# Input projection from x before its division by the row rms, with 1/rms applied by VectorE

## The reference

```python
def rmsnorm(x, g):
    xf = x.astype(jnp.float32)
    y = xf * lax.rsqrt(jnp.mean(xf * xf, axis=-1, keepdims=True) + EPS)
    return (y * g.astype(jnp.float32)).astype(x.dtype)
...
        u = rmsnorm(h, pre_mix_g[i])
        proj = u @ w_in[i]
        q, k, v, u_pool, u_conv = jnp.split(proj, splits, axis=-1)
...
        o_attn = stick_breaking_attention(q.reshape(heads), k.reshape(heads), v.reshape(heads))
        o_pool = multiscale_pool(u_pool, w_pool[i], pool_scale[i])
        o_conv = conformer_conv(u_conv, w_dw[i], b_dw[i], conv_ln_g[i], conv_ln_b[i], w_pw[i])
```

## Time and profile before

| | us |
|---|---|
| Runs, median of 3 | 1078.55 (1078.52 to 1079.44) |
| Span of the profiled execution, first to last instruction | 1076.4 |
| Median less that span | 2.15 |
| TensorE busy | 1065.8 (99%) |
| VectorE busy | 875.0 (81%) |
| ScalarE busy | 589.9 (55%) |

### The profile page before, as it was taken

The page is one execution under the profiler, slowest core; times in us unless marked ns, Lnnn a source line. Parts: engine busy times, 40 slices in busy tenths (PEclk is TensorE's granted clock), DMA queues, the critical chain, the costliest instruction groups (busy, mean ns, idle before and its releaser), DMA issues. The chain is left out here.

```text
span 1076.4 us, 15278 instructions
## 1 busy us (share of the span) xinstructions
PE 1065.8 (99%) x5757; PEld 923.4 (86%) x5757; DVE 875.0 (81%) x1113; ACT 589.9 (55%) x724; POOL 27.2 (3%) x46
## 2 busy tenths in 40 slices
PE   9999999999999999999999999999999999999996
PEld 8999999999888888888888888888888888888885
DVE  6699987637646887899899998998998888777787
ACT  6554454736555566565565555655555555554553
POOL 4000001101000000000000000000000000000000
PEclk9999999999999999999999999999999999999999
DMA  8655535444386485665756665666657666656554
GB/s 277 211 177 169 165 117 158 138 137 138 115 298 215 136 276 185 223 195 177 234 179 194 213 194 182 213 186 224 190 182 228 217 202 199 198 195 217 199 198 180
DMA packets 113207, 208.05 MB, mean 193 GB/s; under 512 B 9184, under 2 KB 46496, under 8 KB 111856
## 3 DMA queue, kind: packets, MB, share of 16 engines
q1 hardware_dynamic: 111952, 201.49, 58.9%
q10 hardware_dynamic: 608, 4.20, 0.9%
q0 software_dynamic: 576, 1.40, 0.4%
HBM read 202.86 MB, written 4.19 MB: 192 GB/s over the span
## 5 line engine op out<-in xcount | busy, mean ns | idle before, releaser
L550 ACT ACTIVATE w_hi<-raw 128x1024 fp32r<-128x1024 f32 x326 | 341.6, 1059 | 263.6 <-PE ps L1703 173.1
L903 DVE TENSOR_TENSOR w_lo<-raw,w_hi 128x1024 fp32r<-128x1024 f32 x326 | 395.1, 1227 | 97.2 <-ACT w_hi L550 96.6
L1701 PE MATMUL ps<-w_hi,uf 128*128 128x512 f32 x524 | 205.3, 392 | 0.1
L1703 PE MATMUL ps<-w_hi,uf 128*128 128x512 f32 x524 | 204.1, 389 | 0.0
L1702 PE MATMUL ps<-w_lo,uf 128*128 128x512 f32 x524 | 203.9, 389 | 0.0
L1365 PE MATMUL ps<-u,w_hi 128*128 128x272 f32 (+1 forms) x544 | 158.8, 292 | 0.0
L1367 PE MATMUL ps<-u,w_hi 128*128 128x272 f32 (+1 forms) x544 | 155.9, 287 | 0.0
L1368 PE MATMUL ps<-u,w_lo 128*128 128x272 f32 (+1 forms) x544 | 155.7, 286 | 0.0
L834 ACT CAST t_hi<-tx 128x1024 fp32r<-128x1024 f32 x84 | 87.0, 1048 | 56.0 <-DVE tx L1203 28.6
L1703 PEld LDWEIGHTS ps<-w_hi,uf 128*128 128x128 f32 x524 | 98.4, 188 | 20.7
L1701 PEld LDWEIGHTS ps<-w_hi,uf 128*128 128x128 f32 x524 | 98.4, 188 | 20.4 <-issue 0.5
(11 more groups left out here) (273 smaller groups left out, 1427.1 us busy)
## 6 DMA issues: line engine op xcount, KB each, us to landing
raw<-in_w_gate SPq DMA_DIRECT2D x176, 256.0 KB, 3.0
raw<-in_w_up SPq DMA_DIRECT2D x176, 256.0 KB, 3.6
raw<-in_w_down SPq DMA_DIRECT2D x88, 512.0 KB, 4.1
raw<-in_w_in SPq DMA_DIRECT2D x72, 512.0 KB, 3.6
raw<-in_w_out SPq DMA_DIRECT2D x32, 512.0 KB, 4.6
arena<-in_x SPq DMA_DIRECT2D x2, 1024.0 KB, 6.0
arena<-in_x ACTq DMA_DIRECT2D x2, 1024.0 KB, 9.4
out<-h2rows SPq DMA_DIRECT2D x2, 1024.0 KB, 5.5
```

The costliest lines, as they stand in the source:

```text
L550: act.activation(w_hi[:, slot, :], raw[:, slot, :], ACT.Copy).then_inc(hi_done, 1)
L903: dve.tensor_tensor(w_lo[:, slot, :], raw[:, slot, :], hi_view(w_hi[:, slot, :]), ALU.subtract).then_inc(lo_done, 1)
L1701: pe.matmul(o, a[0], b[0], start=start, stop=False)
L1703: return pe.matmul(o, a[1], b[0], start=False, stop=stop)
```

## The change

x is loaded in four column pieces of 512 KB, each right behind one of the first four weight chunks. The pieces are turned and multiplied by the gain without 1/rms, each piece while the chunk before it is being multiplied. The squares are taken later: at `q = 4` both engines sum their halves, at 5 ScalarE makes 1/rms and VectorE three small diagonal tiles, and ahead of chunk 5 TensorE multiplies them by ones, which puts 1/rms of every token on all partitions (`rb`, copied by ScalarE at `q = 8`). Every block of the projection, the meta tokens' too, is then multiplied by `rb` as VectorE moves it out of PSUM. ScalarE no longer evicts any; its sigmoid works in place on the gate that VectorE has moved. The product `a_s * sg` moves one chunk later. Of the ones matmuls 24 calls become 10 behind the first nine. GpSimd's work on the meta tokens goes to VectorE, and its two loads of small weights wait for the last piece of x.

```diff
+            x_rows = x[0].rearrange("(m p) d -> p m d", p=P)
...
                         load(win_v, s * CK, col + i * BLK, q, s, wait=q >= WSLOTS)
+                        if q < CK:
+                            cols = slice(s * QUART, (s + 1) * QUART)
+                            sp_eng.dma_start(xr[:, 0:NQ, cols], x_rows[:, :, cols]).then_inc(x_landed[s], 16)
...
+                if q == WSLOTS:
+                    for m in range(NQ):
+                        row_halves(m)
+                if q == WSLOTS + 1:
+                    act.wait_ge(ss_dve, NQ + 1)
+                    inv_rms(r0[:, 0:NQ], ss0[:, 0:NQ], D, r0_done)
+                if q == R_KEPT:
+                    act.wait_ge(rb_made, 1)
+                    act.copy(rb, ps[:, 4, 0:TOK]).then_inc(rb_done, 1)
...
-                        act.wait_ge(chunks_used, e + 1)
-                        act.activation(sg, ps[:, 2:4, 0:TOK], ACT.Sigmoid).then_inc(gate_sig, 1)
+                        act.wait_ge(gate_kept, i + 1)
+                        act.activation(sg, sg, ACT.Sigmoid).then_inc(gate_sig, 1)
                         act.preload_act_table_set("natural_log_exp_and_others")
-                    if e == Q_POOL + (i + 1) * CK - 1:
-                        act.wait_ge(chunks_used, e + 1)
-                        b = pool_bank[i]
-                        act.copy(pu[:, 2 * i:2 * i + 2, :], ps[:, b:b + 2, 0:TOK]).then_inc(pu_kept, 1)
...
+            def scaled_out(dst, bank, done):
+                dve.tensor_tensor(dst, ps[:, bank:bank + 2, 0:TOK], r_both, ALU.mult).then_inc(done, 1)
...
+            for c in range(CK):
+                split(c)
+                input_tiles(range(c * CK, (c + 1) * CK))
...
                 split(q)
+                e = q - WSLOTS
+                if q == WSLOTS:
+                    row_halves()
+                if q == WSLOTS + 1:
+                    token_diagonals()
...
+                    if e == Q_CONV + 2 * i * CK + 2 * CK:
+                        dve.wait_ge(a_kept, i + 1)
+                        dve.wait_ge(gate_sig, i + 1)
+                        dve.tensor_tensor(glu[:, 2 * i:2 * i + 2, GP:GP + TOK], a_s, sg, ALU.mult).then_inc(glu_done, 1)
+                    if e == Q_CONV + 2 * i * CK + 2 * CK - 1:
...
+                        scaled_out(sg, 2, gate_kept)
+                    if e == Q_POOL + (i + 1) * CK - 1:
+                        dve.wait_ge(chunks_used, e + 1)
+                        scaled_out(pu[:, 2 * i:2 * i + 2, :], pool_bank[i], pu_kept)
...
+                        scaled_out(vb[g % 2][:, :, 0:TOK], 2, v_kept)
...
+                            dve.scalar_tensor_tensor(qb[g % 2], ps[:, 4, :].rearrange("p (m t) -> p m t", m=2), DH ** -0.5,
+                                                     r_x, ALU.mult, ALU.mult).then_inc(q_kept, 1)
+                        else:
+                            scaled_out(kb[g % 2][:, :, 0:TOK], 0, k_kept)
...
+                if q == R_AT:
+                    pe.wait_ge(rd_step, NQ + 1)
+                    pe.matmul(ps[:, 4, 0:META], ones, r_meta, start=True, stop=True, skip_group_check=True)
+                    for m in range(NQ):
+                        mm = pe.matmul(ps[:, 4, META + m * P:META + (m + 1) * P], ones, r_diag[:, m, :],
+                                       start=True, stop=True, skip_group_check=True)
+                    mm.then_inc(rb_made, 1)
```

More of the change, by code:

```diff
@@ L315, in build_trunk @@
         hi_done, lo_done, chunks_used = sem("hi_done"), sem("lo_done"), sem("chunks_used")
-        x_landed = [sem(f"x_landed{m}") for m in range(3)]
+        x_landed, meta_landed = [sem(f"x_landed{c}") for c in range(CK)], sem("meta_landed")
         grow_landed, vec_landed, sw_landed, gbc_landed, stored = (
@@ L398, in _ @@
         def _(sp_eng):
-            sp_eng.dma_start(xr[:, 2, 0:D // MSEG], meta.rearrange("t (s c) -> (t s) c", s=MSEG)).then_inc(x_landed[2], 16)
-            for m in range(NQ):
-                sp_eng.dma_start(xr[:, m, :], x[0, m * P:(m + 1) * P, :]).then_inc(x_landed[m], 16)
+            sp_eng.dma_start(xr[:, 2, 0:D // MSEG], meta.rearrange("t (s c) -> (t s) c", s=MSEG)).then_inc(meta_landed, 16)
+            x_rows = x[0].rearrange("(m p) d -> p m d", p=P)
             def load(src, kt, n0, q, slot, kts=CK, cols=BLK, wait=True):
@@ L907, in split @@
                 split_lo(q, q % WSLOTS)
-            for m in range(NQ):
-                dve.wait_ge(x_landed[m], 16)
-                dve.scalar_tensor_tensor(xs[:, m, 0:HALF], xr[:, m, 0:HALF], 1.0, xr[:, m, 0:HALF], ALU.mult, ALU.mult,
-                                         accum_out=ssx[:, m, 0:1]).then_inc(ss_dve, 1)
-                dve.wait_ge(ss_dve, 2 * m + 1)
-                dve.wait_ge(ss_act, m + 2)
-                dve.tensor_tensor(ss0[:, m:m + 1], ssx[:, m, 0:1], ssx[:, m, 1:2], ALU.add).then_inc(ss_dve, 1)
@@ new lines, in token_diagonals @@
+            def token_diagonals():
+                dve.wait_ge(r0_done, 2)
+                dve.tensor_scalar(r_meta, blk.rearrange("p (t s) -> p t s", s=MSEG)[:, :, 0], r0[:, 2:3], 1.0 / MSEG,
+                                  ALU.mult, ALU.mult).then_inc(rd_step, 1)
+                for m in range(NQ):
+                    dve.tensor_scalar(r_diag[:, m, :], ident, r0[:, m:m + 1], None, ALU.mult).then_inc(rd_step, 1)
+            r_both = rb.rearrange("p (a t) -> p a t", a=1).to_broadcast([P, 2, TOK])
@@ L1029, in _ @@
                     head_pair_out(PAIR_AT[q - VALUES - LAG])
-                for i in range(2):
-                    if q - 4 == Q_CONV + 2 * i * CK + 2 * CK - 1:
-                        dve.wait_ge(a_kept, i + 1)
-                        dve.wait_ge(gate_sig, i + 1)
-                        dve.tensor_tensor(glu[:, 2 * i:2 * i + 2, GP:GP + TOK], a_s, sg, ALU.mult).then_inc(glu_done, 1)
                 for n in TAPS_AT.get(q, ()):
@@ L1470, in first_proj @@
                         pe.wait_ge(lo_done, q + 1)
+                    if k == CK - 1 and q < CK - 1:
+                        turn_rows(q + 1)
                     pe.wait_ge(u_lo, kt + 1)
```

200 lines of the change are left out of this document (76 added, 124 removed).

## The result

The changed kernel takes **1082.78 us** (median of six runs; five lie from 1082.15 to 1083.05, with 1082.67 as their median, and one of 5150.12 is left out of the comparison). The kernel before took 1079.10 beside it, so the ratio is 1.0033, interval 1.0023 to 1.0044: 3.7 us slower. I had forecast 1081.0 in a range of 1077.5 to 1083.5, with "slower" as the likeliest. The profiled execution took 1082.61 with a span of 1080.9; the span before was 1076.4.

What follows compares the result with a forecast made beforehand. TensorE was taken to bound the kernel, through its first product, own work and waits. Terms -3.1 + 1.1 + 2.8 + 0.7 + 0.9 = +2.4 on a 1076.4 span, plus 2.15 to the median, gave 1081.0 us; range 1077.5 to 1083.5.

Steps and rivals of the forecast that it cites:

- What bounds the kernel: Whole span: the moment of TensorE's first product plus TensorE's own work; only moving that, added work or waits change the time.
- First product 9.1, chunk 5 at 28.5, gain 3.1: Start: first product near 9.1 us instead of 14.39, chunk 5 at 28.5 instead of 31.65, so 3.1 us gained.
- The wait for 1/rms, 0.4: Ahead of chunk 5: TensorE waits 0.4 us for VectorE's small diagonals, bounds 0 and 1.5.
- An eviction lasts 0.72 and occupies 0.64: VectorE moving a block out of PSUM: lasts 0.72 us, occupies 0.64, bounds 0.51 and 0.93.
- The windows, 1.1: Pooling mix behind chunk 27: TensorE waits for VectorE's windows, a loss of 1.1 us.
- The first k block, 2.8: First scores: VectorE must split chunk 39 before evicting the k block, so TensorE loses 2.8 us.
- The exponentials of pair 1, 0.7: Values of pair 1: the v block at chunk 43 stands ahead of the masking, without slack, a loss of 0.7 us.
- The later k blocks, 0.9 in all: First scores of the three later groups: 0.3 us lost at each k block, 0.9 in all.
- The clock: Rival: the wait at the k block drops TensorE to 1.2 GHz, a chunk lasts 6 not 3 us; 1084, chance 0.08.
- The sign of being wrong: Refuted if VectorE idles ahead of its splits of chunks 13 to 27, or TensorE waits nowhere behind 30 us.
- VectorE keeps up: Rival: VectorE's chain is shorter, so the mix and first k block come in time; 1077.0, chance 0.17.
- Late pieces: Rival at the start: x's pieces land late, or the first product comes at 10 us; 1082.0, chance 0.14.

Runs made afterwards that it cites:

- e10: The changed kernel, unedited, profiled once more; 1082.59 us.
- e1: Changed kernel's new start alone: ScalarE evicts the projections as before, and the division by rms is left out; 1075.52 us, ratio 0.9968.
- e5: Changed kernel with eight filter taps moved from blocks 24 to 27 and 34 to 37 to blocks 48 and 49; 1078.52 us, ratio 0.9994.
- e3: Changed kernel with each k block evicted one chunk number earlier on VectorE; 1078.92 us, ratio 0.9999.
- e4: Changed kernel with eight matmuls on ones ahead of the first scores, in the wait for the k block; 1080.92 us, ratio 1.0018.
- e6: Changed kernel with four instead of ten of the second ones matmuls; 1081.92 us, ratio 1.0024.
- e2: Kernel before, old start, with VectorE evicting the blocks and multiplying by a tile of ones; 1087.49 us, ratio 1.0072.
- e11: The kernel of e6, unedited, profiled once more; 1080.84 us.
- e7: Changed kernel with the edits of e3, e5 and e6 together, and the v block moved behind the masking; 1075.23 us, ratio 0.9963.

## Why the prediction was right, point by point

The range held the time, and the sign and the mechanism of the waits were as forecast. The time came 1.8 us above the forecast. Of this, 0.55 is the starting point: 1078.55 was the median of three runs, and the kernel before took 1079.10 beside the changed one. The change itself was forecast at +2.4 and measured at +3.7. There the term left out, the clock (+1.5 to +2.7), is larger than the whole gap, and terms sized too high made up for a part of it. That the total came as near as it did is partly luck.

- **What bounds the kernel.** Right. Every wait of TensorE is in the total, and no other engine's time is: ScalarE lost 10 us of busy time and nothing came of it.
- **First product 9.1, chunk 5 at 28.5, gain 3.1.** Right for a like start: e10 has 9.26 and 28.47 against 14.39 and 31.65, a gain of 3.18 (the terms written down add up to 8.97, and not 9.1). In the first profile they were 10.55 and 29.78, because everything ahead of the turning ran slower: the first nine ones calls by 0.54 us, the small products behind them by 0.40 and the ten calls by 0.35. I had priced them by the 0.116 us of the earlier trace rows, taken when the clock was up. The landing of x's first piece was wrong: forecast at 6.3 to 6.7, it came between 7.45 and 8.16 in all ten profiles of the new start. That cost nothing with ten ones calls, which in e10 held TensorE until 7.70; with four calls TensorE waited for the piece (0.43 to 1.72 us). Chunk 5 lay from 31.65 to 32.36 in the two profiles of before and from 28.47 to 29.78 in the two of after, so "3.1 earlier" is 1.9 to 3.9 by the pair one takes, and 3.6 by the medians of e1 and before.
- **The wait for 1/rms, 0.4.** It was 0.14 us in both profiles of after and 0.15 at most (e5).
- **An eviction lasts 0.72 and occupies 0.64.** Right: 714 ns, and at chunk 27 the first tap follows 0.64 behind its start (92.01 to 92.65). The Trainium skill ("Perfetto Trace Analysis", Optimizing Scalar/DVE Operations) gives VectorE about 60 ns of access overhead on SBUF and 125 on PSUM. The same 544 elements took 726 ns from SBUF alone and 714 with one operand in PSUM, so no such difference shows here.
- **The windows, 1.1.** 72.18 - 70.85 = 1.33, of which the row names 1.01 as a wait.
- **The first k block, 2.8.** 6.87 - 4.11 = 2.76 in the three profiles with the clock at its upper level; the row says 2.70. That VectorE's place in order and backlog, and not the multiplication's rate, sets it is shown by e3 and e5. VectorE had no idle time from its split of chunk 20 to this block.
- **The exponentials of pair 1, 0.7.** 4.72 - 4.09 = 0.63 in e4 and e6; only 0.28 to 0.29 in after, e10 and e2, the three profiles in which a slow stretch had already held TensorE back.
- **The later k blocks, 0.9 in all.** Some 0.5: 0.16 us each at the second and third group (58.93 - 58.62 = 0.31 together), and at the fourth, behind chunk 71, a wait of 0.36 us, of which 0.2 is left in the total (812.9 against 812.7). The second group, whose rows I had read, was sized at twice what it cost.
- **The clock.** This is the term that was wrong. I named it as a rival with a chance of 0.08 and 3 us, and left it out of the sum. Both profiles of after have it, for 1.5 and 2.7 us. "The clock never falls" was a misreading: a 9 in a slice of 27 us can hide up to 5.4 us at half the clock. The trace of the kernel before does show one, behind its last matmul, which ended at 1068.26 (stretches as above):

```profile
1070.00:1072.00 2.00, 0.00 (x0) 0.00 (x0) 2.00 (x3) 0.00 (x0) 0.00 (x0) 1.00 0.22 86
1072.00:1074.00 2.00, 0.00 (x0) 0.00 (x0) 0.60 (x2) 0.00 (x0) 0.00 (x0) 0.66 1.00 391
1074.00:1076.00 2.00, 0.00 (x0) 0.00 (x0) 0.00 (x0) 0.00 (x0) 0.00 (x0) 0.50 0.42 138
```

It came at 1072.64, after 4.38 us without a matmul. So the trace on record had an idle time with a fall, 1.6 times as long as the wait that I forecast, and none that told how much shorter one may be. The Trainium skill ("TensorE: Matmul & The Clock Gate", HAM oscillation) says that long idle gaps of TensorE let the clock go back to half rate; the falls of after, e10 and e2 agree, e6 and e11 with the same gap show none, and the rule deserved more than 0.08. With the rival's 3 us my sum gave 1084; measured was 1082.78, because the clock cost less than 3 us, and the exponentials and the later k blocks less than their terms.

- **The sign of being wrong.** I had written that idle time of VectorE ahead of its splits of chunks 13 to 27 would refute me. There is one, of 1.52 us ahead of the split at 70.56, chunk 20. It is the detour over the sigmoid that my own chain has at this place, so the sign was worded too widely; ahead of the other splits of that stretch there is none.

With the measured terms up to chunk 71, e10 against the first profile of before: -3.18 + 1.34 + 2.76 + 2.71 + 0.29 + 0.32 = 4.24, and chunk 71 is at 267.97 against 263.70, 4.27 later.

*VectorE keeps up* didn't happen in this order: TensorE waited for the windows and for two k blocks. How close it was is shown by e7, which moves eight taps and the k and v blocks and has none of the waits. *Late pieces* was half right: no product waits for a piece of x in the changed kernel, but a first product later than 10 us did come.

## What to carry to other kernels

An operation given to a less loaded engine is priced by where it stands in that engine's order, not by its length: eighteen evictions of 0.7 us (fourteen of line 900 and four q blocks) cost 6.2 to 7.4 us in one order, 1.5 to 2.7 of it by the clock, and nothing in another (e7), with eight taps and the k and v blocks moved. Find on the receiving engine what is due first behind it, put the eviction ahead of work that nobody waits for, and lighten the stretch ahead of each due time. A wait on TensorE costs more than its length once the clock falls behind it (2.7 us of wait cost 1.5 to 2.7 more), so price that case at full before calling it unlikely.

## What the runs showed of the hardware that I had not expected

- A wait of TensorE of 2.70 us was followed by 3.41 us at the 1.2 GHz level in one profile of the changed kernel and in e2, by 6.83 us in the other, and by none in both profiles of e6. Behind the last matmul the clock fell in all thirteen profiles, after 1.97 us (e6) to 5.29 us (e2). What decides it within one kernel isn't settled; with 0.90 us of idle time ahead of the scores (e4) none of eleven runs was as slow as the changed kernel.
- Two executions of the changed kernel, 1.3 us apart at the first product, ended within 0.02 us of each other, since the earlier one had the longer slow stretch. In these two a steady total hid two effects of opposite sign.
- The clock's first rise came between 4.08 and 7.08 us in thirteen profiles, by the trace's record of clock changes. In the changed kernel's start, two 128x128 turns took 0.69 us with a rise at 6.9 or later and 0.44 with an earlier one. The first 18 ones matmuls took 4.21 us with a rise at 5.29 or later and 3.62 to 3.76 with one at 4.35 or earlier. What sets its moment isn't settled.
